# Levels one to four of a triangular inverse, multiplied as diagonal 32x32 blocks

## The reference

```python
def step(state, inp):
    r_t, w_t, k_t, v_t, a_t, b_t = inp
    sa = jnp.einsum('bhvk,bhk->bhv', state, a_t)
    state = (state * w_t[:, :, None, :] + sa[..., None] * b_t[:, :, None, :]
             + v_t[..., None] * k_t[:, :, None, :])
    return state, jnp.einsum('bhvk,bhk->bhv', state, r_t)
```

## Time and profile before

| | |
|---|---|
| time, median of 3 runs | 2663.88 us (2660.07 to 2666.73) |
| profiled execution, its own time | 2657.73 us |
| its span, first to last instruction | 2655.9 us |
| mean granted TensorE clock | 0.984 |
| busy: TensorE, VectorE, ScalarE, GpSimd | 95%, 48%, 40%, 30% |
| matmul records of the levels' products: t (XI,MA), xt (XIT,TS), x (TS,XIT) | 1280, 1280, 1024 |

### The profile page before, as it was taken

The page is one execution under the profiler, slowest core; times in us unless marked ns, Lnnn a source line. Parts: engine busy times, 40 slices in busy tenths (PEclk is TensorE's granted clock), DMA queues, the critical chain, the costliest instruction groups (busy, mean ns, idle before and its releaser), DMA issues.

```text
span 2655.9 us, 50606 instructions
## 1 busy us (share of the span) xinstructions
PE 2513.7 (95%) x19738; PEld 2026.1 (76%) x19738; DVE 1266.6 (48%) x2016; ACT 1053.4 (40%) x1848; POOL 808.3 (30%) x342
## 2 busy tenths in 40 slices
PE   7999999999999999999999999989988989898997
PEld 6888886878787887787778887878776668666676
DVE  3222225445353627455342222247756764575775
ACT  4222234343343434564242222233246642425662
POOL 3444443323333233224434444422220002233002
PEclk9999999999999999999999999989999999999999
DMA  4333332222222122112322233311110002122002
GB/s 139 95 95 95 99 99 91 74 72 73 78 60 89 55 90 79 56 48 83 129 93 91 91 94 96 106 52 56 55 40 25 1 1 63 48 65 70 17 2 71
DMA packets 52009, 188.53 MB, mean 71 GB/s; under 512 B 5760, under 2 KB 6016, under 8 KB 51712
## 3 DMA queue, kind: packets, MB, share of 16 engines
q1 hardware_dynamic: 50688, 181.74, 22.3%
q10 hardware_dynamic: 1152, 4.26, 0.5%
HBM read 183.88 MB, written 2.10 MB: 70 GB/s over the span
## 4 chain that ended last, share of the span: by engine, by line
issue 71%; POOL 14%; PE 11%; DVE 2%; ACT 1%; POOLq 1%; DMA 0%; DVEq 0%; SPq 0%; ACTq 0%
POOL WLO L2616 14%; PE psum L319 2%; PE psum L320 2%; PE psum L321 2%; PE psum L2377 1%; PE psum L2356 1%; PE psum L2392 1%; PE psum L2362 1%; DVE MX L2447 0%; DVE RN L2080 0%; POOLq L2613 0%; ACT PX L2414 0%; PE psum L2193 0%; DMA RAW<-in_wstream 0%; POOLq L2615 0%
## 5 line engine op out<-in xcount | busy, mean ns | idle before, releaser
L2616 POOL TENSOR_TENSOR WLO<-RAW,WHI 128x1024 fp32r<-128x1024 f32 x334 | 803.2, 2406 | 1820.4 <-ACT WHI L307 1820.2
L307 ACT ACTIVATE WHI<-RAW 128x1024 fp32r<-128x1024 f32 x336 | 355.8, 1059 | 1089.0 <-PE psum L321 806.9
L319 PE MATMUL psum<-HHI,WHI 128*128 128x512 f32 x848 | 339.5, 400 | 17.9 <-DVE HLO L491 11.5
L320 PE MATMUL psum<-HLO,WHI 128*128 128x512 f32 x848 | 335.9, 396 | 0.0
L321 PE MATMUL psum<-HHI,WLO 128*128 128x512 f32 x848 | 335.7, 396 | 0.0
L319 PE MATMUL psum<-H2HI,WHI 128*128 128x512 f32 (+1 forms) x536 | 199.5, 372 | 23.7 <-DVE CIN L2115 9.5
L319 PEld LDWEIGHTS psum<-HHI,WHI 128*128 128x128 f32 x848 | 159.7, 188 | 59.2 <-issue 12.0
L320 PE MATMUL psum<-H2LO,WHI 128*128 128x512 f32 (+1 forms) x536 | 193.0, 360 | 0.0
L321 PE MATMUL psum<-H2HI,WLO 128*128 128x512 f32 (+1 forms) x536 | 192.7, 360 | 0.0
L320 PEld LDWEIGHTS psum<-HLO,WHI 128*128 128x128 f32 x848 | 159.8, 188 | 38.8 <-issue 1.2
L321 PEld LDWEIGHTS psum<-HHI,WLO 128*128 128x128 f32 x848 | 159.8, 188 | 38.6
(11 more groups left out here) (425 smaller groups left out, 5001.7 us busy)
## 6 DMA issues: line engine op xcount, KB each, us to landing
RAW<-in_wstream SPq DMA_DIRECT2D x336, 512.0 KB, 3.6
X<-in_xT SPq DMA_DIRECT2D x8, 256.0 KB, 6.4
out_T<-OUT SPq DMA_DIRECT2D x4, 512.0 KB, 2.7
W3S<-in_lora ACTq DMA_DIRECT2D x5, 384.0 KB, 3.3
XC<-in_ctxT ACTq DMA_DIRECT2D x1, 1024.0 KB, 7.3
TRIG<-in_trig ACTq DMA_DIRECT2D x1, 960.0 KB, 9.3
FCC<-in_first SPq DMA_DIRECT2D x1, 576.0 KB, 8.3
LVL<-in_levels SPq DMA_DIRECT2D x1, 384.0 KB, 8.7
```

Source lines behind the costliest of these rows:

```text
L307: act.activation(WHI[:, q % 2, :], RAW[:, q % 2, :], ACT.Copy).then_inc(rounded, 1)
L319: pe.matmul(out, tile_of(WHI, slot, u), hi(kt), start=first and last[0], stop=False)
L320: pe.matmul(out, tile_of(WHI, slot, u), lo(kt), start=False, stop=False)
L2616: pool.tensor_tensor(WLO[:, s, :], RAW[:, s, :], WHI[:, s, :].bitcast(F32), ALU.subtract)\
```

## The change

Levels 1 to 4 give up the full 64x64 products. The blocks that the masked copies pick up at these levels lie within the diagonal 32x32 blocks, and so do all the blocks they are made from; each_quarter multiplies only these: for each chunk four matmuls of 32 rows, 32 weight columns and 32 moving columns, at partitions 0, 32, 64 and 96, one for each 32x32 diagonal block of the two heads. A product becomes 32 matmuls in place of 16. The rest of the PSUM bank keeps what it held, is copied to TS as before, and is never picked up. Level 5 keeps the 64x64 products. Nothing else is changed: not the copies, the semaphores, the order or the transfers.

```diff
+        QUARTER = CHUNK // 2
+
+        def each_quarter(pe, out, lhs, rhs):
+
+            pe.sem_inc(tensor_ready)
+            for n in range(CHUNKS):
+                for z in range(P // QUARTER):
+                    s, c = slice(z * QUARTER, (z + 1) * QUARTER), z % 2 * QUARTER
+                    mm = pe.matmul(out[s, n * CHUNK + c:n * CHUNK + c + QUARTER], lhs[s, n, c:c + QUARTER], rhs[s, n, c:c + QUARTER],
+                                   start=True, stop=True)
+            return mm
...
+                def inner_products(l, out, lhs, rhs, name):
+
+                    if 2 << l <= QUARTER:
+                        each_quarter(pe, out, lhs, rhs).then_inc(*S.inc(name))
+                    else:
+                        unit_products(unit(out), mat(lhs), mat(rhs), name)
...
-                    unit_products(unit(d.B[0]), mat(d.MA1), mat(d.XI), f"t{l}_{p}")
+                    inner_products(l, d.B[0], d.MA1, d.XI, f"t{l}_{p}")
...
-                        unit_products(unit(d.B[1]), mat(d.XIT), mat(d.TS), f"x{l}_{p}")
-                    unit_products(unit(d.B[2]), mat(d.TS), mat(d.XIT), f"xt{l}_{p}")
+                        inner_products(l, d.B[1], d.XIT, d.TS, f"x{l}_{p}")
+                    inner_products(l, d.B[2], d.TS, d.XIT, f"xt{l}_{p}")
```

## The result

The changed kernel takes 2725.40 us (median of 4 runs, 2722.61 to 2728.99) against 2663.58 for the kernel before beside it: a ratio of 1.0239, 95% interval 1.0226 to 1.0251, so 62 us slower. The forecast was 2641. The profiled execution took 2724.3 us, its span 2722.5, at a mean granted clock of 0.964 (before 2655.9 and 0.984).

The account below looks back on a forecast made before the run. TensorE, busy 95% of the span, was taken as the bound: 24 x 0.33 - 0.8 = 7.2 us a round, capped by the weight stream at 5.7, 23 us in four rounds, so 2641 us; range 2630 to 2670.

Parts of the forecast that it names:

- The product's own time: Levels 1 to 4: a product takes 0.60 us instead of 0.93, four row groups working at once; 0.33 us off each.
- Changes of shape: Seven new borders a round between 32-row and 64-row products on TensorE cost 0.12 us each, 0.8 us a round.
- The feeding: TensorE is handed a product's 128 instructions at 5 ns each, 0.64 us, going by two loads 0.04 us apart after a wait.
- The coinciding starts: Two matmuls both starting at 563.14 were read as each head's half of the array running its own sequence, 58 ns a record.
- The prediction's own sign for bad feeding: In the next profile, products of levels 1 to 4 taking 1.6 us or more would show the feeding was wrong.
- fed too slowly: Rival: TensorE gets instructions at 14.5 ns, a product takes 1.87 us, +93 us, 2757 us; chance 0.16.
- The weight stream as the cap: Streamed weights' slot cycle of 7.25 us makes TensorE wait about 1.5 us a round, capping the gain at 5.7 us a round.
- "TensorEngine Tiling (Array Packing)", Performance Considerations: Rule behind the rival "no change": 32 moving columns save nothing, products stay near 0.9 us, +3 us, 2667 us; chance 0.13.
- Back-to-back issue gap, read over the whole array: Milder form of slow feeding: starts at least 25 ns apart, 1.6 us a product, +67 us; no chance of its own.

Follow-up runs that it names:

- the tail: Kernel before, plus TensorE alone running 32x32 f32 matmuls of constants after the last output, in a straight line and in loops; one profiled execution, 2897.17 us.
- two-block run: Changed kernel with two of the four diagonal 32x32 blocks left out of each product of levels 1 to 4: 2652.86 us, ratio 0.9968.
- easing the stream: GpSimd makes the remainder WLO for half the columns, on the kernel before (2641.57 us) and with two blocks a product left out (2634.24 us).

## Why the prediction was wrong, point by point

- **The product's own time: right in size, its reason only in part.** 0.60 us start to start. That each tile runs its own sequence fits (two blocks a product: 32 records in 0.53 us, 33 ns for each of a tile's 16); that it takes four row groups does not, since tiles of 64 rows in two row groups took 0.61. Loads take 110 and 113 ns (x and xt; t, which more often meets the lower clock, 132), matmuls 198 and 202 (220), where 109 and 192 were forecast.
- **Changes of shape: fits as far as seen.** From t2_0 (508.17) to m2_1 (508.88) it is 0.71 us, 0.11 more than a product. Not tested by itself. The run with one t product short, -2 us where the array saves 5, agrees.
- **The feeding: the step that failed.** "128 instructions at 5 ns are 0.64 us" was right for one product and was taken for all. The row behind it, two loads 0.04 us apart after a wait, shows what a full store hands over. The step asked how fast TensorE takes instructions and not how fast they arrive: 14.3 ns each (the tail, one packet of 256 in 3.67 us). The 14.5 ns of the kernel before came close to it by luck: it was the array's pace of 16 records at 58 ns. The coinciding starts showed nothing about supply. The prediction's own sign for bad feeding, products of 1.6 us or more, missed it too: products took 0.60 at the full clock, and the waits stood as stops in and between them. The right sum goes by stretches: over a level step before, 19.5 ns an instruction, above 14.3; over the changed level stage 3,588 in some 35 us of array time (42.6 less 7.2), under 10 ns each, so that even on the average the supply needs 51 us (3,588 x 14.3, less what is in store at the start) where the stage before took 42.6; and over the four short products in a row 512 in 2.4 us, 4.7 ns each, where a full store covers some 400. The average explains 9 of the 15.3 us of a round, the rest goes with the bursts and the clock; the two were not told apart.
- **The rival "fed too slowly"** named the right cause with too little chance (0.16) and the wrong sum (+93 us). It charged every product 1.87 us, as if nothing were stored during the modulations. The level stages lost 15 us a round where it said 23.
- **The clock: not in the prediction.** No term and no rival had it; the 1.00 in the earlier trace rows was taken as given. By the sum above 43 us of the rounds' busy time come from it. Shown: busy time exceeds the work by 36 to 43 us where the granted clock of the rounds is 0.92 to 0.94, by 22 at 0.97, by 12 at 0.98. Shown by the two-block run: where TensorE hardly waits this is time lost. Not shown: what it cost the change, where well over half of it lies in stretches that the supply bounded anyway. The run with added gaps shows that gaps between full-size products do not bring it on to this extent, and the tail that 32x32 matmuls with hardly a gap need not; which property of small products and which stops do it together stays open.
- **The weight stream as the cap: not reached, and wrong where the level stage did get shorter.** In after ScalarE's WHI copies wait for TensorE (10.19 us before the copy at 536.46), not for the DMA. In the two-block kernel some copies do wait for the DMA (2.60 us before the one at 540.20), but easing the stream changed the gain by 0.6 us only.
- **The Trainium skill.** "TensorEngine Tiling (Array Packing)", Performance Considerations, would have kept a product at 0.9 us: the trace disagrees, 0.60. "TensorE: Matmul & The Clock Gate", Back-to-back issue gap, read over the whole array gave +67 us and came near the result for another reason: inside a product records start 0.60 / 64 = 9.4 ns apart, not 25. The page that bears on it I did not weigh: "Runtime: NRT & Kernel Launch", Instruction fetch mechanics, has instructions come in blocks of 16 KiB, 256 instructions, through a queue of the sequencer's own into a store. The trace agrees, 24 packets for 6,144 instructions. The page calls the cost of it mostly hidden; here it is hidden down to 14.3 ns an instruction and not below. It gives TensorE's store 2,048 instructions; in the tail some 400 ran before the first gap, and a loop of 2,048 starved in every pass, so here the measurement decides.

## What to carry to other kernels

Count the instructions of every stretch, not only their array time: an edit that cuts a matmul into smaller ones is free only while each stretch stays above what the supply brings (here 14.3 ns an instruction, with some 400 in store), and both count, the average and the worst run of consecutive instructions. If columns are to be taken off, do it at the same number of instructions; here that cost nothing and gained next to nothing. And when TensorE's work is made smaller and sparser, look at the granted clock as well: in the two-block kernel it took back up to 36 of the 38 us that the array had saved. But do not add busy time stretched by the clock to waits for another bound as if each could be won back alone.

## What was not expected of the hardware

- New instructions reach TensorE at one packet of 256 every 3.67 us with no other traffic on this core's queues; a loop whose body is 512 instructions runs, after its first pass, without any gap at 10.5 ns a record, while a body of 2,048 is brought anew in each pass.
- With 32x32 products in two row groups and 4.2 us of issue waits in four rounds, the granted clock was at its 1.2 GHz level for part of each level stage (0.93 over the rounds), and the same product took 0.87 us in place of 0.53. In the tail 32x32 matmuls in four row groups kept 1.00 for 28 us. In the kernel before, with 64x64 products, 16 added gaps of 1.61 us brought it only to 0.98.
- Tiles that share their rows but not their output partitions work at once: a product of 32 matmuls of 64 rows and 32 columns took 0.61 us, as one of 32x32 tiles.
- The supply does not run on ahead without limit: with only x and xt short, no packet of instructions came between 523.5 and 531.8 us, while two t products took 3.68 us at the lower clock in place of 2.08.
